# Feed-forward on one core: down-projection two iterations behind the up-projection, weight units reordered

## What is computed

```python
def conv_ffn(h, w_up, conv_w, conv_b, w_down):   # h: 256 x 1024, D_FF = 2816
    u = h @ w_up                                  # 256 x 5632: gate and value
    up = jnp.pad(u, ((0, 0), (pad, pad), (0, 0))) # pad = 1
    u = sum(up[:, t:t + S] * conv_w[t] for t in range(3)) + conv_b
    gate, val = jnp.split(u, 2, axis=-1)
    return (jax.nn.silu(gate) * val) @ w_down

h = h + conv_ffn(rms_norm(h, ffn_norm[i]), ffn_w_up[i], ffn_conv_w[i], ffn_conv_b[i], ffn_w_down[i])
```

## Time and profile before

| | us |
|---|---|
| three runs of the kernel | 1124.91 (median), 1124.73, 1128.6 |
| span of the profiled execution, first to last instruction | 1121.9 |
| TensorE busy in it | 1080.1 (96%) |
| VectorE busy | 745.6 (66%) |
| ScalarE busy | 584.3 (52%) |
| GpSimd busy | 220.0 (20%) |

### The profile page before, as it was taken

One profiled execution on the slowest core, in us unless ns is written; L12 is line 12 of the kernel. 1 busy time (PEld: TensorE's weight loads), 2 busy tenths in 40 slices (PEclk: granted clock), 3 DMA queues, 4 the chain that ended last, 5 costly groups with the idle time before them and its releaser, 6 DMA issues.

```text
span 1121.9 us, 17467 instructions
## 1 busy us (share of the span) xinstructions
PE 1080.1 (96%) x6920; PEld 957.5 (85%) x6920; DVE 745.6 (66%) x964; ACT 584.3 (52%) x884; POOL 220.0 (20%) x180
## 2 busy tenths in 40 slices
PE   8999999999997999999999997989999999999997
PEld 7767799989895777799989895789899988999996
DVE  5966667787876755467777876765565577555553
ACT  5656774545455646464545445643353466444442
POOL 1311032223133243333132233231000000000000
PEclk9999999999998999999999998999999999999999
DMA  8623344554553542253645544564443346656541
GB/s 303 236 69 120 113 151 145 194 182 155 188 172 128 188 148 78 73 168 123 209 164 183 187 151 149 165 211 152 150 138 127 113 132 217 206 178 196 179 148 38
DMA packets 114644, 177.51 MB, mean 158 GB/s; under 512 B 3419, under 2 KB 85524, under 8 KB 114580
## 3 DMA queue, kind: packets, MB, share of 16 engines
q1 hardware_dynamic: 114004, 175.05, 47.0%
q10 hardware_dynamic: 576, 1.57, 0.4%
HBM read 175.56 MB, written 1.05 MB: 157 GB/s over the span
## 4 chain that ended last, share of the span: by engine, by line
PE 61%; DVE 14%; issue 13%; ACT 9%; POOL 2%; DMA 1%; ACTq 1%; DVEq 0%; SPq 0%; POOLq 0%
PE ps L1824 56%; DVE wlo L1211 4%; DVE scr L1365 3%; ACT scr L837 3%; ACT whi L702 3%; DVE scr L1357 2%; DVE scr L1372 2%; DVE scr L1379 1%; PE ps L1898 1%; ACT ohi L848 1%; PE ps L2297 1%; PE ps L1944 1%; POOL xn L628 0%; PE ps L2070 0%; DMA raw<-in_swa_w_qkv 0%
## 5 line engine op out<-in xcount | busy, mean ns | idle before, releaser
L1824 PE MATMUL ps<-xhi,whi 128*128 128x256 f32 x1248 | 356.0, 285 | 0.0
L1824 PE MATMUL ps<-xlo,whi 128*128 128x256 f32 x1248 | 353.7, 283 | 0.0
L1824 PE MATMUL ps<-xhi,wlo 128*128 128x256 f32 x1248 | 353.7, 283 | 0.0
L1211 DVE TENSOR_TENSOR wlo<-raw,whi 128x2048 fp32r<-128x2048 f32 x124 | 284.2, 2298 | 86.8 <-ACT whi L702 86.2
L702 ACT ACTIVATE whi<-raw 128x2048 fp32r<-128x2048 f32 x150 | 284.5, 1908 | 59.2 <-PE ps L1824 36.3
L1824 PEld LDWEIGHTS ps<-xhi,whi 128*128 128x128 f32 x1248 | 239.6, 192 | 4.2 <-issue 1.4
L1824 PEld LDWEIGHTS ps<-xlo,whi 128*128 128x128 f32 x1248 | 239.7, 192 | 1.2
L1824 PEld LDWEIGHTS ps<-xhi,wlo 128*128 128x128 f32 x1248 | 239.6, 192 | 0.0
L595 POOL TENSOR_TENSOR wlo<-raw,whi 128x2048 fp32r<-128x2048 f32 x26 | 122.9, 4727 | 295.9 <-ACT whi L702 295.9
L1824 PE MATMUL ps<-whi,ohi 128*128 128x512 f32 x368 | 128.3, 407 | 21.8 <-DVE olo L1383 21.8
L837 ACT ACTIVATE scr<-scr,cwT 128x256 f32<-128x256 f32 x88 | 48.1, 594 | 154.5 <-DVE scr L1357 154.5
(11 more groups left out here) (189 smaller groups left out, 1212.2 us busy)
## 6 DMA issues: line engine op xcount, KB each, us to landing
raw<-in_ffn_w_up SPq DMA_DIRECT2D x44, 1024.0 KB, 5.1
raw<-in_w_in SPq DMA_DIRECT2D x23, 1024.0 KB, 5.3
raw<-in_ffn_w_down SPq DMA_DIRECT2D x22, 1024.0 KB, 4.9
raw<-in_w_mlp_in SPq DMA_DIRECT2D x16, 1024.0 KB, 5.3
raw<-in_w_mlp_out SPq DMA_DIRECT2D x16, 1024.0 KB, 4.9
raw<-in_diff_w_qkv SPq DMA_DIRECT2D x11, 1024.0 KB, 5.6
raw<-in_ple_w_gate SPq DMA_DIRECT2D x8, 1024.0 KB, 5.0
raw<-in_swa_w_qkv SPq DMA_DIRECT2D x6, 1024.0 KB, 5.2
```

The costliest lines, as they stand in the source:

```text
L1211: dve.tensor_tensor(wlo[:, u % RING, :], raw[:, u % RAW, :], whi[:, u % RING, :].bitcast(F32), ALU.subtract).then_inc(lo_ready, 1)
L1824: return pe.matmul(o, l, r, start=start, stop=stop, skip_group_check=True)
```

## The change

The down-projection is moved one iteration back: iteration `it` of the loop does the up-projection `it` and the down-projection `it - 2`, and the loop is over iterations 2 to 9. TensorE's order becomes

```diff
-POOL_UNITS = [U0[f"ffn{l}"] + n for l in range(2) for n in (*range(1, 29, 3), 30, 32, 34)]
+POOL_UNITS = [U0[f"ffn{l}"] + n for l in range(2) for n in (*range(3, 31, 3), 32)]
```

On ScalarE:

```diff
-                    def hidden_hi(buf, wait):
-
-                        act.wait_ge(hid_ready[l], wait)
-                        act.activation(ohi[:, 2 * buf:2 * buf + 2, :].rearrange("p a c -> p (a c)"), hid[:, buf, :],
+                    def hidden_hi(it, i=None):
+
+                        act.wait_ge(hid_ready[l], at(it + 1, FFN_TURN, i))
+                        o = 2 * (it % 4)
+                        act.activation(ohi[:, o:o + 2, :].rearrange("p a c -> p (a c)"), hid[:, it % 2, :],
                                        ACT.Copy).then_inc(hhi_ready[l], 1)
...
-                        if after is None:
+                        if units == 3:
                             keep_ahead(ug + 2, i)
-                        else:
-                            act.wait_ge(weights_used, after)
-                        hidden_hi(buf, at(it + 1, FFN_TURN, i))
+                        hidden_hi(it, i)
...
-                    hidden_hi(0, 1)
+                    hidden_hi(0)
+                    iteration(1, u0 + 2, 2)
                     with act.Fori(0, 8 // FFN_TURN) as i:
                         for n in range(FFN_TURN):
-                            iteration(1 + n, i)
-                    split[0] = u0 + 25 + RING
-                    iteration(9, None, u0 + 26)
-                    iteration(10, None, u0 + 28, u0 + 31)
+                            iteration(2 + n, u0 + 4 + 3 * n, 3, i)
+                    split[0] = u0 + 27 + RING
+                    iteration(10, u0 + 28, 2)
                     ahead(u0 + 30)
                     ahead(u0 + 31)
```

On TensorE:

```diff
                     def down(ud, it, start, stop, i=None):
                         pe.wait_ge(hlo_ready[l], at(it + 1, FFN_TURN, i))
                         for t in range(T):
-                            tm_half(ud, t, ohi, olo, 2, 2 * t, start, stop, None, i, k0=2 * (it % 2))
-
-                    def iteration(it, i=None):
-                        ug = u0 + 3 * it - 1
+                            tm_half(ud, t, ohi, olo, 2, 2 * t, start, stop, None, i, k0=2 * (it % 4))
+
+                    def ups(it, ug, i=None):
                         for gv in range(2):
+                            if it > 1:
+                                pe.wait_ge(scaled[l], at(2 * (it - 2) + gv + 1, 2 * FFN_TURN, i))
                             up(ug + gv, it % 2, gv, i)
-                        down(ug + 2, it - 1, False, False, i)
...
+                    ups(1, u0 + 2)
                     with pe.Fori(0, 8 // FFN_TURN) as i:
                         for n in range(FFN_TURN):
-                            iteration(1 + n, i)
-
-                    for n, it in enumerate((9, 10)):
-                        for gv in range(2):
-                            up(u0 + 26 + 2 * n + gv, it % 2, gv)
+                            ups(2 + n, u0 + 4 + 3 * n, i)
+                            down(u0 + 6 + 3 * n, n, False, False, i)
+                    ups(10, u0 + 28)
                     down(u0 + 30, 8, False, False)
```

More of the change, by code:

```diff
@@ L657, in _ @@
                         rope_add(6, s // 2, HALF)
-                split_lo(U0["ffn1"] + 1)
                 norm_rstd(4)
@@ L1379, in mult, with hidden_lo, iteration @@
                         dve.tensor_tensor(hid[:, buf, :], sgl[:, buf, :], cgv[:, buf, 1, :], ALU.mult).then_inc(hid_ready[l], 1)
-                    def hidden_lo(buf, n):
-                        dve.wait_ge(hhi_ready[l], n)
-                        dve.tensor_tensor(olo[:, 2 * buf:2 * buf + 2, :].rearrange("p a c -> p (a c)"), hid[:, buf, :],
-                                          ohi[:, 2 * buf:2 * buf + 2, :].rearrange("p a c -> p (a c)").bitcast(F32),
+                    def hidden_lo(it, i=None):
+                        o = 2 * (it % 4)
+                        dve.wait_ge(hhi_ready[l], at(it + 1, FFN_TURN, i))
+                        dve.tensor_tensor(olo[:, o:o + 2, :].rearrange("p a c -> p (a c)"), hid[:, it % 2, :],
+                                          ohi[:, o:o + 2, :].rearrange("p a c -> p (a c)").bitcast(F32),
                                           ALU.subtract).then_inc(hlo_ready[l], 1)
-                    def iteration(it, i=None, ug=None):
-                        buf = it % 2
-                        straight = ug is not None
-                        ug = ug if straight else u0 + 3 * it - 1
+                    def iteration(it, ug, units=3, i=None):
                         for gv in range(2):
@@ L1393, in iteration @@
                             taps(it, gv, i, ug)
-                        mult(buf, at(2 * it + 2, 2 * FFN_TURN, i), at(it + 1, FFN_TURN, i))
-                        if not straight:
+                        mult(it % 2, at(2 * it + 2, 2 * FFN_TURN, i), at(it + 1, FFN_TURN, i))
+                        if units == 3:
                             keep_ahead(ug + 2, i)
-                        hidden_lo(buf, at(it + 1, FFN_TURN, i))
+                        hidden_lo(it, i)
                     ahead(u0)
@@ L1404, in ffn @@
                     mult(0, 2, 1)
-                    hidden_lo(0, 1)
+                    hidden_lo(0)
+                    iteration(1, u0 + 2, 2)
                     with dve.Fori(0, 8 // FFN_TURN) as i:
                         for n in range(FFN_TURN):
-                            iteration(1 + n, i)
-                    split[0] = u0 + 25 + RING
-                    iteration(9, None, u0 + 26)
-                    iteration(10, None, u0 + 28)
+                            iteration(2 + n, u0 + 4 + 3 * n, 3, i)
+                    split[0] = u0 + 27 + RING
+                    iteration(10, u0 + 28, 2)
                     ahead(u0 + 30)
@@ L2201, in ffn @@
                         mm(ps[:, bank, 0:P], identb[:, :], zerob[:, :], True, False)
+                    ups(1, u0 + 2)
                     with pe.Fori(0, 8 // FFN_TURN) as i:
                         for n in range(FFN_TURN):
-                            iteration(1 + n, i)
-                    for n, it in enumerate((9, 10)):
-                        for gv in range(2):
-                            up(u0 + 26 + 2 * n + gv, it % 2, gv)
+                            ups(2 + n, u0 + 4 + 3 * n, i)
+                            down(u0 + 6 + 3 * n, n, False, False, i)
+                    ups(10, u0 + 28)
                     down(u0 + 30, 8, False, False)
                     pe.wait_ge(hlo_ready[l], 10)
-                    last_rows(u0 + 31, ohi, olo, (2, 0), 2 + 3 * l, (5, 6, 7),
+                    last_rows(u0 + 31, ohi, olo, (2, 4), 2 + 3 * l, (5, 6, 7),
                               [(0, 0, 0), (0, 0, 1), (0, 1, 0), (1, 0, 0), (1, 0, 1), (1, 1, 0), (0, 1, 1), (1, 1, 1)],
```

26 lines of the change are left out of this document (12 added, 14 removed).

## The result

| | before | changed |
|---|---|---|
| median of five runs, us | 1124.91 | 1132.25 |
| lowest and highest, us | 1124.62, 1128.6 | 1130.65, 1132.65 |
| span of the profiled execution, us | 1121.9 | 1130.4 |
| mean granted clock in it | 0.990 | 0.986 |

The ratio is 1.0051, with a 95% interval of 1.0041 to 1.0062: the changed kernel is slower by 4.6 to 7.0 us.

What follows compares the result with a forecast made beforehand. The prediction took a ring of ScalarE, GpSimd and VectorE, 17.75 us an iteration, as the bound, with TensorE following. Terms 2.5 + 1.8 + 1.6 + 0.3 = +6.2 us on 1124.9 gave 1131.1 us, range 1125.8 to 1135.5.

Steps and rivals of the forecast that it cites:

- The ring: Feed-forward loop: ScalarE, GpSimd and VectorE in program order hold each iteration at 17.75 us; the change gains 0 there.
- the wait really goes: Loop: the period falls to TensorE's 17.05 us, 9.8 us off; chance 0.07 for a time below 1119.3 us.
- Unit 1 at the start: Start of each feed-forward: VectorE's split of unit 1 delays TensorE's transposes, +2.5 us in layer 0, +1.8 in layer 1.
- the boundary costs are hidden: Start of the feed-forwards: idle time or a later gap swallows unit 1's split, leaving 1126.8 us; chance 0.15.
- First and last iterations: Feed-forward body: +1.2 us for the straight iteration now first, -0.4 in iteration 0; +1.6 us for two layers.
- The end: End of each feed-forward: unit 34's split on VectorE ahead of the residual additions, +0.3 us for two layers; idling 5.0 us.
- The clock: Ends of the feed-forwards: shorter idling might keep TensorE's clock up, gaining up to 4 us; 0 was taken.
- below 1 nowhere but at the ends: Sign of being wrong: a granted clock below 1 anywhere but at the end of the two feed-forwards.
- The rival held that it might fall behind the new stalls: Start of the feed-forwards: the clock falls at the new stalls, 2.2 us lost per layer, up to 1138.7 us; chance 0.10.
- it may come back later too: Ends of the feed-forwards: the clock falls later and returns later, all 18 matmuls at 1.2 GHz, 1.6 us more a layer.
- The bound by which the sum took 0: End of each feed-forward: transposes 2.0 us earlier would find the residual addition, now 2.2 us later, not done; gain 0.
- TensorE's own queue: Loop: two more waits make TensorE's iteration 18.05 us, +0.3 in each of 16, 1135.9 us; chance 0.06.

Runs made afterwards that it cites:

- The first experiment: The changed kernel with only unit 1's split in each feed-forward given back from VectorE to GpSimd: 1126.65 us, ratio 0.9999 to the kernel before.

## Why the prediction was right, and where not

Predicted 1131.1 us, measured 1132.25, within the range, and on the side that had 0.56, if only just: by the ratio the change costs 5.7 us, where the line between slower and the same was drawn at 5.6 and the sum had +6.2. Step by step:

- **The ring (gain on the path 0).** Right. 17.73 us against the 17.75 foretold, and the rows named for it are there: `wlo` in place of `olo`, 2.90 us once, then 0.38 to 0.57 where TensorE waits. What it rested on was the row that is missing from the earlier trace rows, VectorE waiting for `ps`; as soon as the ring was opened by another route, that row appeared. The rival "the wait really goes" had put the freed loop at TensorE's 17.05 us an iteration, and it measures 16.98; only the way to it was another than this change.
- **Unit 1 at the start (+2.5, +1.8).** Right in place and size: 2.49 and 1.83 us. The rival "the boundary costs are hidden" fell.
- **First and last iterations (+1.6).** Iteration 0 gave -0.28 (-0.4 foretold), the body behind it +1.08 (+1.2). In layer 1 they are -0.26 and +0.58, +0.32 together in place of +0.8; there one loop iteration of the kernel before happened to be 0.34 us longer. The first experiment puts this term and the next together at -1.1 to +0.9 us, where I had +1.9: too dear by a microsecond or more. The two traces have more, 1.1 us here and about 0.5 in the next term; why is open.
- **The end (+0.3).** The last idle time was to be 5.0 us and is 4.66. The transposes behind it came 0.57 and 0.98 us later still, but 0.2 and 0.8 us of that was given back within the next stages, so that little reaches the end. It was not the addition behind two splits that held them, as the term has it: in layer 0 the addition was done at about 355.6, and the transposes followed their last matmul without a gap at 356.27. It was the clock (next step).
- **The clock (0 taken, and "below 1 nowhere but at the ends").** This is the step that failed. The rival held that it might fall behind the new stalls, with 0.10. It fell behind the 2.33 us one and cost 1.5 us there (2.2 priced), but not behind the 1.68 us one. My evidence against it was a stretch with 1.74 us of idling at full clock, and that was the exception: the same stretch, with nearly the same idling ahead of it, runs at half clock in the changed kernel and in all eight experiments. One execution had been read as a rule. The sign of being wrong was badly drawn too, since the kernel before has the half clock itself in places that I had not listed, from 11.6 to 14.8 us and in its last 4 us. The clock also fell behind the 2.90 us waits in both loops, where it costs nothing, since TensorE waits for the ring anyway.

  At the ends of the feed-forwards nothing was gained by shorter idling: the half clock of 342.6 to 349.4 became one of 348.2 to 355.0, equally long. It begins in the idle time, and with the idle time shorter more of it lies on the matmuls, in layer 0 for 5.5 us of them in place of 4.4. That is the case which the prediction kept for its range ("it may come back later too", up to 1.6 us a layer), and it gave 0.57 and 0.98. The Trainium skill's rule that was weighed there (TensorE: Matmul & The Clock Gate, section on HAM oscillation), by which idle gaps are to be avoided since they take the clock down, agrees in direction with the fall behind the stall; the gain of up to 4 us that a shorter gap might have given by it did not come. The bound by which the sum took 0 does hold, as the first experiment shows: there the half clock at the end of layer 0 was half as long, 346.5 to 349.9, and the transposes then waited for the addition:

```profile
352.45 0.65 PE L1897 MATMUL ps<-tab,h 128*128 128x128 f32 x4 [0.23 <-DVE h L1270]
```

- **TensorE's own queue (rival, 0.06).** Fell: a period of 17.73 us leaves no room for the 0.3 us an iteration that it asked for.

The term that was too dear and the clock that was left out have opposite signs and about the same size. That the sum is closer than its parts is luck; the ring and unit 1's two stalls, 4.32 of the 5.7 us, are not.

## What to carry to other kernels

A long wait in a list is a gain only if the engine that is waited for has something to gain from its release. Here TensorE waited for VectorE and nobody waited for TensorE, so moving TensorE's consumption back only changed which partner of the same ring was named. Look for the operation in the ring that takes longer than its own work elsewhere (`olo`, 4.33 against 0.69 us): handing a split of 2.3 us from GpSimd to VectorE took 2.25 us out of VectorE's iteration of 17.75 us, brought TensorE to its own 16.98, and took 2% off the kernel.

And what an engine is spared in one place must be asked of the place it is moved to: unit 1 on VectorE cost the whole loss of this change, because it stands ahead of an addition for which TensorE waits.

## What the runs showed of the chip that I had not expected

- How complete the stop is. Sixteen GpSimd operations whose results nobody reads cost the kernel 45.9 us, and VectorE's split is longer by 3.40 of the 3.61 us that it runs. I had left open anything from 3.5 to 4.7 us, after the 4.72 us of GpSimd's split; that the useless one takes 3.61 us for as many elements (both its operands are the same tensor, the split's are two) was not expected, and no run shows why.
- The granted clock behind a stall is not the same in each profile. Six profiled kernels have the 2.33 us stall ahead of layer 0's transposes; in four the half clock begins between 0.2 us before the stall's end and 0.5 us behind it (at 146.8, 147.5, 146.1 and 147.3 us of their spans), in the two with GpSimd's idle operations it does not fall there at all. Each kernel was profiled once, so this alone does not tell kernel from execution; but the five executions of the changed kernel have mean granted clocks from 0.985 to 0.993, so it differs between executions of one kernel too. Nor does the length of the last stall decide. Behind the single 1.7 us stall ahead of layer 1's transposes the clock never fell; behind the two idle pieces of the stretch of the earlier trace rows, the second 1.74 to 1.76 us long, it fell in nine profiles of ten. A term of this kind is thus a chance rather than a sum, and is better carried in the range.
